# A float32 streaming-encoder block: the slots of the split weight slabs moved off the streamed operands' place in 512 bytes

## What is computed

```python
h = h + 0.5 * _swiglu(_rmsnorm(h, ffn1_norm[l]), ffn1_w_gate[l], ffn1_w_up[l], ffn1_w_down[l])
h = h + _mixer(_rmsnorm(h, mix_norm[l]), w_in[l], ...)   # GLA, Mamba-2 SSD, chunked attention, gated and merged
h = h + 0.5 * _swiglu(_rmsnorm(h, ffn2_norm[l]), ffn2_w_gate[l], ffn2_w_up[l], ffn2_w_down[l])
return _rmsnorm(h, final_norm)
```

## Time and profile before

| | us |
|---|---|
| median of 3 runs (1828.5 to 1829.5) | 1829.39 |
| the profiled execution, its own time | 1830.17 |
| its span in the trace | 1828.4 |
| PE busy | 1798.8 |
| PEld busy | 1503.0 |
| DVE busy | 961.5 |
| ACT busy | 622.6 |

### The profile page before, as it was taken

One profiled execution on the slowest core, in us unless ns is written; L12 is line 12 of the kernel. 1 busy time (PEld: TensorE's weight loads), 2 busy tenths in 40 slices (PEclk: granted clock), 3 DMA queues, 4 the chain that ended last, 5 costly groups with the idle time before them and its releaser, 6 DMA issues.

```text
span 1828.4 us, 26276 instructions
## 1 busy us (share of the span) xinstructions
PE 1798.8 (98%) x9852; PEld 1503.0 (82%) x9852; DVE 961.5 (53%) x1360; ACT 622.6 (34%) x986; POOL 115.9 (6%) x109
## 2 busy tenths in 40 slices
PE   7999999999999999999999999999999999999997
PEld 5888888887888888888988888887888888888885
DVE  6444443379888888632544445555334544444333
ACT  4222322344444444332333344443222323222221
POOL 4111100000110110000000000000000011111000
PEclk9999999999999999999999999999999999999998
DMA  4323233321222222233222222222233233232331
GB/s 156 104 92 96 99 103 104 103 92 58 81 69 69 69 79 70 70 105 102 84 88 72 81 92 80 91 83 78 93 94 101 92 95 101 92 103 92 104 108 64
DMA packets 47353, 164.92 MB, mean 90 GB/s; under 512 B 5520, under 2 KB 6672, under 8 KB 47296
## 3 DMA queue, kind: packets, MB, share of 16 engines
q1 hardware_dynamic: 43584, 158.10, 26.8%
q10 hardware_dynamic: 3712, 6.03, 1.1%
HBM read 162.01 MB, written 2.10 MB: 90 GB/s over the span
## 4 chain that ended last, share of the span: by engine, by line
PE 76%; issue 19%; DVE 3%; POOL 1%; DMA 0%; ACT 0%; POOLq 0%; DVEq 0%; SPq 0%; ACTq 0%
PE G L538 37%; PE G L580 12%; PE I L538 9%; PE G L554 7%; PE I L902 1%; POOL hid L460 1%; PE I L936 1%; PE I L912 1%; PE G L767 1%; PE I L709 1%; PE I L717 1%; PE I L727 1%; DVE UL L1499 1%; PE I L670 0%; PE I L872 0%
## 5 line engine op out<-in xcount | busy, mean ns | idle before, releaser
L1483 DVE TENSOR_TENSOR WL<-RAW,WH 128x1024 fp32r<-128x1024 f32 x297 | 374.4, 1263 | 295.6 <-ACT WH L1031 286.6
L1031 ACT CAST WH<-RAW 128x1024 fp32r<-128x1024 f32 x297 | 309.3, 1046 | 222.5 <-PE I L538 126.4
L538 PE MATMUL G<-UH,WH 128*128 128x512 f32 x696 | 172.9, 390 | 0.0
L538 PE MATMUL G<-UL,WH 128*128 128x512 f32 x696 | 171.9, 389 | 0.0
L538 PE MATMUL G<-UH,WL 128*128 128x512 f32 x696 | 171.9, 389 | 0.0
L538 PEld LDWEIGHTS G<-UH,WH 128*128 128x128 f32 x696 | 130.6, 188 | 28.0 <-issue 1.0
L538 PEld LDWEIGHTS G<-UL,WH 128*128 128x128 f32 x696 | 130.6, 188 | 27.1
L538 PEld LDWEIGHTS G<-UH,WL 128*128 128x128 f32 x696 | 130.6, 188 | 27.1
L538 PE MATMUL G<-NH,WH 128*128 128x512 f32 x448 | 113.6, 396 | 0.0
L538 PE MATMUL G<-NL,WH 128*128 128x512 f32 x448 | 110.7, 389 | 0.0
L538 PE MATMUL G<-NH,WL 128*128 128x512 f32 x448 | 110.6, 389 | 0.0
(11 more groups left out here) (309 smaller groups left out, 2548.1 us busy)
## 6 DMA issues: line engine op xcount, KB each, us to landing
RAW<-in_slabs SPq DMA_DIRECT2D x297, 512.0 KB, 3.4
h<-in_x SPq DMA_DIRECT2D x4, 512.0 KB, 7.3
bias<-in_rel ACTq DMA_DIRECT2D x16, 128.0 KB, 3.0
out_y<-h ACTq DMA_DIRECT2D x8, 256.0 KB, 2.2
bias<-in_rel ACTq DMA_DIRECT2D x16, 112.0 KB, 2.7
cst<-in_cst SPq DMA_DIRECT2D x1, 168.0 KB, 3.7
ut<-in_wgk SPq DMA_DIRECT2D x3, 32.0 KB, 8.7
```

Of the source, the lines that this page charges most:

```text
L538: ins = mm(dst, W[:, n.slot, (k - k0) * P:(k - k0 + 1) * P], R[:, k, :], start=begin and which == 0 and k == k0, stop=end and which == 2 a ...
L1031: nc.scalar.copy(WH[:, n.slot, :], RAW[:, n.slot, :]).then_inc(split_hi, 1)
L1483: V.tensor_tensor(WL[:, n.slot, :], RAW[:, n.slot, :], WH[:, n.slot, :].bitcast(F32), ALU.subtract).then_inc(split_lo, 1)
```

## The change

```diff
 RING = 3
+STEP = 4
...
         RAW = sb("RAW", [P, RING, SLAB])
-        WH = sb("WH", [P, RING, SLAB], F32R)
-        WL = sb("WL", [P, RING, SLAB], F32R)
+        WH = sb("WH", [P, RING, SLAB + STEP], F32R)
+        WL = sb("WL", [P, RING * (SLAB + STEP) + 2], F32R)[:, 2:].rearrange("p (s c) -> p s c", s=RING)
+        sb("offset", [P, 96])
...
-                nc.scalar.copy(WH[:, n.slot, :], RAW[:, n.slot, :]).then_inc(split_hi, 1)
+                nc.scalar.copy(WH[:, n.slot, 0:SLAB], RAW[:, n.slot, :]).then_inc(split_hi, 1)
...
-                V.tensor_tensor(WL[:, n.slot, :], RAW[:, n.slot, :], WH[:, n.slot, :].bitcast(F32),
+                V.tensor_tensor(WL[:, n.slot, 0:SLAB], RAW[:, n.slot, :], WH[:, n.slot, 0:SLAB].bitcast(F32),
                                 ALU.subtract).then_inc(split_lo, 1)
```

## The result

The changed kernel takes 1853.88 us (median of 4 runs, 1853.64 to 1855.21), the kernel before beside it 1829.45 us (4 runs). The ratio is 1.0135, 95% interval [1.0124, 1.0147]: slower by 24.4 us. The forecast was 22 us the other way; the first rival had said 1851.

A forecast was written before the change was run, and what follows sets the result against it. The prediction took PE to bound the kernel, through its matmuls' start-to-start distance. From 1830.2 us it took 22 for matmuls, nothing for ACT, DVE and DMA: 1808, as median 1807; range 1783 to 1858.

The forecast's parts named there:

- the first rival: Slab matmuls: new places conflict more and the steady state is lost; 1851 us, all a step up 1874; slower 0.37.
- What bounds the kernel: Whole kernel: PE busy 1798.8 of 1828.4 us, so time is the count of matmuls times their start-to-start distance.
- the addition of 13.3 ns: Each matmul at 2.4 GHz takes 13.3 ns beyond its columns, 226.7 against 213.3; read as operands' places conflicting.
- `LR` row: Four matmuls streaming `LR` 192 bytes off loaded `WGK`, 96 partitions: 233 ns each, 6.7 more than the steady distance.
- `after_r` row: Matmuls loading `after_r` 32 bytes off `MSH`: 233 ns, but the next 8 average 230; place not separable from start-up.
- The clock row: At 1.2 GHz starts lie 427 ns apart, exactly 512 columns, nothing added; taken as the addition belonging to the load.
- The second rival: Slab matmuls: place does not matter, 13.3 ns is a fixed cost of changing weights; 1829 us, same 0.17.
- The price of one: 6643 changed slab matmuls: half go one step of 6.7 ns down, the rest stay; 22 us saved.
- more room below than above: Argument for faster, 0.46: the addition has 13.3 ns of room below, against 6.7 shown above by one row.
- two ways: 27 ns a pass, 3 passes a slab, 257 slabs, 21 us; or half the changed matmuls a step up, 22 us.
- theory B: Experiments' expectation: place does not matter, each pass between places costs some 8 matmuls at 230 ns; remainders alone about 1847 us.
- ACT and DVE: Rounding and remainder write the same bytes to other places; costed at nothing, covered by three slabs of lead.

The follow-up runs named there:

- The scan: A separate kernel of float32r matmuls alone, back to back, 32 per place, loaded operand stepped 4 bytes against the streamed: 226.7 ns at 0, 233.4 at +64 (512 columns).
- the prices of the scan: A second matmul-only kernel, each place entered from several others; passing back to place 0 cost over 226.7: 39 ns from +72 and +88, 4 from +104.
- The two programs: The kernel before with all six slots moved to one common place off the streamed operands: +16 bytes, 1857.03 us; +156 bytes, 1884.31 us.

## Why the prediction was wrong

- *What bounds the kernel, and that only the distance from start to start can matter:* right. PE's added busy time of 24.6 us is the loss.
- *That the addition of 13.3 ns depends on the relative place:* right. The scan, and the kernel with all slots at 64, show it. Both rows with places apart had said it truly. In the `LR` row, 192 bytes off read the other way round is +64 in a period of 256, for which the scan has 233.4 and the row 233; its 96 partitions need not be called on. The `after_r` row at +32, which I put down to start-up, has 233 as well, and the scan 233.3. Both pointed up.
- *The clock row, taken as a stream at half speed beside a load:* read too narrowly. The loads slow down too there: the line below, from the trace before, shows one of 0.33 us at the granted clock of 0.50, against 188 ns at 1.00. So the row doesn't separate the load from the stream.

```profile
433.76 0.33 PEld L681 LDWEIGHTS I<-MSH,after_r 128*128 128x128 f32 x1
```

- *The second rival, that place can't matter,* is refuted for this form (226.7 against 233.3 and more, on matmuls alone with nothing else running). By the rule of the Trainium skill that the prediction names (SBUF — State Buffer, section "Who interferes with whom"), with two independent read ports, place could not matter; the measurement decides otherwise for the distance, and whether the cause lies in the reads is open.
- *"The price of one":* the step that failed. I took half of the changed matmuls one step of 6.7 ns down, 22 us saved. For 512 columns there is no place below 226.6 among 64, and half of the places (32 of 64) settle at 233.0 to 233.7. The 4723 moved matmuls cost 28.5 us / 4723 = 6.0 ns each on the mean, one step up for nearly all. Down was open only for 256 columns, where the chosen places gave 1.5 ns and not the 6.7 that 112 gives.
- *The reason that I gave for faster, "more room below than above":* it took the 13.3 ns for a range within which a place falls by chance. The old place was the lowest distance that any scan or kernel here shows with 512 columns, so there was no room below. The tight 226 and 227 in all stretches, against 230 to 235 in the rows after a disturbance, already hinted that equal places are a good regime.
- *The first rival* had the result to 3 us, by two ways that each hold a part. That it came so near is in part luck, since neither way is what happened. A step up for half of the matmuls was too few. The price of 27 ns a pass, three times a slab, does not hold in the changed kernel: the only pass back to +0 there costs one matmul at 231, some 4 ns. And there is a third thing in the passes that it lacked: they carry PE from one pattern into another. The run with the rounded slabs alone kept +16 at 227 and lost 7 us; with the remainders at +72 ahead of them the same matmuls run at 233. Where the remainders alone were moved, passes did cost: the 8 matmuls behind the remainders of slots 0 and 1 take 231 ns on the mean while PE comes back to 226.7. That is 39, 39 and 4 ns for the three slots, the prices of the scan from +72, +88 and +104. The sum is 2024 x 6.3 = 12.7 us for the remainders and 257 x 27 ns = 7 us for the passes, against 18.8 us measured; so theory B's agreement with this run holds for its second term alone.
- *ACT and DVE:* right. The median of the remainder (line 1485 now) is 1226 ns for 1225, of the rounding (line 1033) 1048 for 1048. The test by slots that I had named (slot 0 stays, the others change) came out as for "place", with 227.3 in slot 0.
- *The range* ended at 1858 and holds the result only because it took in the first rival; the sign was wrong.

What stays open is the mechanism: what in the chip makes the distance depend on the place. One reading of the trace speaks for the load and the stream beside it. In slot 0 of the changed kernel the first load of the remainder runs beside the last UL matmul, and the distance behind that matmul is already 232 ns, one matmul before the remainder is used:

```profile
37.98 0.19 PEld L540 LDWEIGHTS G<-UL,WH 128*128 128x128 f32 x1
38.20 0.19 PEld L540 LDWEIGHTS G<-UH,WL 128*128 128x128 f32 x1
```

The last UL matmul starts at 38.20 and the first with the remainder at 38.43. Against it: the addition does not shrink steadily with the columns loaded, which speaks against the simple picture of two readers of which one gives way for as long as the other reads. Why the distances lie on steps of 6.7 ns was not tried.

## What to carry to other kernels

Back-to-back float32r matmuls of 512 columns, each with its own load of 128 columns, ran best, and the same in every run, with the loaded and the streamed operand at the same place modulo 256 bytes; keep ring slots at multiples of 256 and put padding in units of that. Where a form streams 256 columns, a different place for that form alone is worth measuring (113.3 against 120.0 ns). When a row shows an addition to the columns, find out by a scan of matmuls alone whether any place has less of it before crediting a change with removing it, and look at runs as well as at means: a program whose runs fall into two groups may have more than one steady pattern.

## What the runs showed of the hardware

- The distance from start to start of float32r matmuls depends on the difference of the two operands' places modulo 256 bytes: in the first scan 226.6 to 237.2 ns with 512 columns (steps of 4 bytes), 113.2 to 123.1 with 256 (steps of 8).
- It has memory: one place can have two or more lasting patterns (+16: 226.7 and 233.3; +156: 226.7 and a cycle with a mean of 243.3; +12: four), kept over more than a thousand matmuls. The two programs in which this was seen also show two run times each (1852 and 1861.5, 1871.7 and 1897.3 us); that the patterns make them is an estimate that fits, 10.1 us for 9.4 and 25.5 for 25.6, and not shown by a profile.
- Passing back to equal places always ended at 226.7 (64 of 64 entries), for 0 to 50 ns by the place left.
- Neither DVE's nor ACT's accesses show in it: the kernel's 233.3 at +64 is the scan's 233.4 with the other engines idle.
